# Hybrid conv / MLA / MoE step on one core: conditioning units moved ahead of the latent weights and of the sum of squares

## The reference, cut to what matters

```python
shift1, scale1, gate1, shift2, scale2, gate2 = split(silu(c_vec) @ w_ada + b_ada, 6)   # w_ada: 1024 x 6144
h = rms_norm(x, norm1) * (1 + scale1) + shift1
conv_in, q_lat, kv_lat, k_rope, gates = split_projection(h @ w_in)      # w_in: 1024 x 3488
...
x = x + gate1 * ((g_conv * conv_out + g_att * att) @ w_out)
h2 = rms_norm(x, norm2) * (1 + scale2) + shift2
x = x + gate2 * hier_moe(h2, ...)       # 16 experts in 4 groups, top 1 group, top 2 experts
```

## Time and profile before

| | |
|---|---|
| median of 3 runs | 1084.63 us (1083.62 to 1086.83) |
| the profiled execution's own time | 1087.17 us |
| its span (first to last instruction) | 1085.4 us |
| TensorE busy (PE) | 975.4 us, 90% |
| VectorE busy (DVE) | 758.0 us, 70% |
| ScalarE busy (ACT) | 514.9 us, 47% |
| chain that ended last, by engine | PE 79%, DVE 10%, issue 5%, ACT 4%, DMA 3% |
| mean granted TensorE clock | 0.934 |

### The profile page before, as it was taken

The page is one execution under the profiler, slowest core; times in us unless marked ns, Lnnn a source line. Parts: engine busy times, 40 slices in busy tenths (PEclk is TensorE's granted clock), DMA queues, the critical chain, the costliest instruction groups (busy, mean ns, idle before and its releaser), DMA issues.

```text
span 1085.4 us, 15630 instructions
## 1 busy us (share of the span) xinstructions
PE 975.4 (90%) x5962; PEld 812.6 (75%) x5962; DVE 758.0 (70%) x1187; ACT 514.9 (47%) x732; POOL 13.3 (1%) x15
## 2 busy tenths in 40 slices
PE   4599999998998798998958999998899969899997
PEld 1388699777997776786837968986699867678775
DVE  0655979556654688898866587975566367898895
ACT  0451633366323475666554244317543157656662
POOL 0100000000000000000010000000000000000000
PEclk8599999998998699999988999999999968999999
DMA  9765265401530776868366426550045047875861
GB/s 379 308 230 217 79 263 210 187 1 40 206 143 1 293 292 248 309 260 336 136 243 262 175 101 245 211 209 34 9 169 205 8 192 288 338 267 213 341 235 58
DMA packets 30249, 215.48 MB, mean 199 GB/s; under 512 B 3553, under 2 KB 3585, under 8 KB 4449
## 3 DMA queue, kind: packets, MB, share of 16 engines
q1 hardware_dynamic: 29808, 213.20, 51.4%
q0 software_dynamic: 368, 1.29, 0.3%
HBM read 212.75 MB, written 1.74 MB: 198 GB/s over the span
## 4 chain that ended last, share of the span: by engine, by line
PE 79%; DVE 10%; issue 5%; ACT 4%; DMA 3%; DVEq 0%; SPq 0%; ACTq 0%; another core or an unknown queue 0%
PE ps L723 56%; PE ps L710 6%; PE ps L734 4%; DMA ring<-wfirst 2%; PE ps L930 2%; PE ps L1024 2%; PE ps L978 2%; ACT w_hi L1332 2%; PE ps L701 1%; PE ps L851 1%; DVE w_lo L594 1%; PE ps L1108 1%; DVE x L1871 1%; DVE rs L1464 1%; PE ps L920 1%
## 5 line engine op out<-in xcount | busy, mean ns | idle before, releaser
L594 DVE TENSOR_TENSOR w_lo<-ring,w_hi 128x2048 fp32r<-128x2048 f32 x96 | 218.6, 2290 | 33.8 <-ACT w_hi L1332 30.4
L1332 ACT ACTIVATE w_hi<-ring 128x2048 fp32r<-128x2048 f32 x96 | 182.5, 1911 | 34.7 <-PE ps L723 30.5
L723 PE MATMUL ps<-h_hi,w_hi 128*128 128x384 f32 x512 | 174.8, 341 | 0.0
L723 PE MATMUL ps<-h_hi,w_lo 128*128 128x384 f32 x512 | 172.0, 336 | 0.0
L723 PE MATMUL ps<-h_lo,w_hi 128*128 128x384 f32 x512 | 171.9, 336 | 0.0
L589 DVE TENSOR_TENSOR w_lo<-ring,w_hi 128x2048 fp32r<-128x2048 f32 x44 | 100.4, 2290 | 50.7 <-ACT w_hi L583 50.7
L583 ACT ACTIVATE w_hi<-ring 128x2048 fp32r<-128x2048 f32 x44 | 83.6, 1909 | 69.1 <-DMA ring<-wpre 34.3
L1529 DVE SCALAR_TENSOR_TENSOR z<-u,par,z 128x399 f32<-128x399 f32 x180 | 104.7, 629 | 1.5
L723 PEld LDWEIGHTS ps<-h_hi,w_hi 128*128 128x128 f32 x512 | 96.1, 188 | 11.2 <-issue 10.4
L723 PE MATMUL ps<-w_hi,hg_hi 128*128 128x512 f32 x256 | 103.8, 405 | 0.0
L723 PE MATMUL ps<-w_hi,hg_lo 128*128 128x512 f32 x256 | 101.3, 396 | 0.0
(11 more groups left out here) (243 smaller groups left out, 1627.0 us busy)
## 6 DMA issues: line engine op xcount, KB each, us to landing
ring<-wpre SPq DMA_DIRECT2D x96, 1024.0 KB, 6.2
ring<-wmoe SPq DMA_DIRECT2D x96, 1024.0 KB, 5.4
ring<-wfirst SPq DMA_DIRECT2D x8, 1024.0 KB, 13.6
x<-x SPq DMA_DIRECT2D x1, 1536.0 KB, 15.5
x_out<-x SPq DMA_DIRECT2D x4, 384.0 KB, 2.3
par<-par_in POOLq DMA_DIRECT2D x3, 367.5 KB, 6.8
const<-const_in SPq DMA_DIRECT2D x1, 314.0 KB, 3.0
ckv_out<-ckvT POOLq DMA_DIRECT2D x2, 64.0 KB, 2.7
```

The costliest lines, as they stand in the source:

```text
L594: return nc.vector.tensor_tensor(out, whole, leading.bitcast(F32), ALU.subtract)
L723: m = mm(out, a, b, start=(start and i == 0 and j == 0), stop=(stop and i == n - 1 and j == 2))
L1332: af(w_hi[m % MOE_PLACES], slot(pre_slot(m)), ACT.Copy).then_inc(split_hi, 1)
```

## The change

The three first conditioning units go to the head of each layer's list, ahead of the two latent units; one is left behind these (before: four). On TensorE the first two are worked ahead of the sum of squares, the third behind it, and the fourth behind latent chunk 3 (before: one behind the sum, three behind chunks 1, 3 and 5). The first unit of a batch gets two waits: for the batch before to have left bank 7 (`adaT_taken`), and for the third of the MoE's last products to have been added (`x_moe`). Nothing on ScalarE or VectorE is changed, nor the number of units or of matmuls.

```diff
-ADA_HEAD = 4
+ADA_AHEAD = 3
+ADA_HEAD = 1
-LAT_ADA = (1, 3, 5)
+LAT_ADA = 3
@@ pre_stream
-    out = [("lat", 0), ("lat", 1)] + [("ada", next(ada)) for _ in range(ADA_HEAD)]
+    out = [("ada", next(ada)) for _ in range(ADA_AHEAD)] + [("lat", 0), ("lat", 1)]
+    out += [("ada", next(ada)) for _ in range(ADA_HEAD)]
@@ ada
-                    if kind == "next" and n == first_unit:
-                        wait_taken(pe, l, "o", TT - 1)
+                    if n == first_unit:
+
+                        pe.wait_ge(adaT_taken, batches_before(l, kind))
+                        if kind == "next":
+                            wait_taken(pe, l, "o", TT - 1)
+                        else:
+                            pe.wait_ge(x_moe, done * KD + (BACK_BANKS.index(ADA_BANK) + 1))
@@ the start of the layer on TensorE
+                ada(PRE[0])
+                ada(PRE[1])
                 square_sum(0)
 
-                units = adas_after("lat", 1)
-                ada(units[0])
+                ada(PRE[2])
                 outs = [begin("lat", t) for t in range(TT)]
...
-                    if c in LAT_ADA:
-                        ada(units[LAT_ADA.index(c) + 1])
+                    if c == LAT_ADA:
+                        for e in adas_after("lat", 1):
+                            ada(e)
```

## The result

The changed kernel takes 1091.23 us, median of 17 runs (1084.98 to 1101.42), against 1084.63 for the kernel before (17 runs, 1080.8 to 1096.08). The ratio is 1.0056, interval 1.0032 to 1.0080: slower by 6.1 us, 3.5 to 8.7. The profiled execution took 1101.42 us, 10 above the median and the longest of the 17, so totals are read beside a second profile (1089.4 us span).

A forecast was written before the change was run, and what follows sets the result against it. TensorE holds 79% of the chain; changes count where the chain leaves it or its work could go elsewhere. +7.56 - 2.00 - 2.00 = +3.56 us on the profiled 1087.17, or +0.33%; on median 1084.63 that gives 1088.2, range 1085.2 to 1091.0.

The forecast's parts named there:

- The landing, +7.56: First layer's start: the latent unit, fourth instead of first, lands 7.56 us later and delays the first latent matmul as much.
- The chunks, -2.00 each: Latent chunks, both layers: two of three conditioning units between chunks go, each saving 1.00 us, so -2.00 per layer.
- The two units ahead of the sum, and the queue behind, 0: Second layer's start and later transfers: units fit TensorE's idle time before the sum of squares, later landings hold nothing up; 0.
- Sharing of the engines: Rival, faster: six transfers land near one another, so list place hardly counts; only -4.00 us remains, 1080.6; chance 0.08.
- VectorE stopping TensorE: Rival, second layer: chunks wait for VectorE's h_lo (slack 0.77 us), so no gain there; +5.56, 1090.2; chance 0.10.
- TensorE waited for h_lo between chunks: Sign at the latent chunks: seeing this wait in the changed profile would show the forecast wrong; no size given.
- The sum of squares as the late one: Rival: the sum, now behind two units, becomes the root's last release; adds some 1 us, 1089.2; chance 0.02.
- The clock: Rival at the latent products: the clock's slow stretch falls otherwise, 1087.0 or 1089.4; chance 0.20, half to each side.

The follow-up runs named there:

- second set: The changed kernel unaltered, timed and profiled again against the kernel before: ratio 1.0036 (1.0011 to 1.0061).
- one unit alone: Kernel before with one conditioning unit ahead of the latent ones in the first layer's list only; one execution, span 1088.2 us.
- first only: Changed kernel with the second layer put back as before, first layer as changed: ratio 1.0057 (1.0022 to 1.0091), median 1091.32 us.
- list only: Changed kernel with both layers' lists as changed but TensorE's order as before: ratio 1.0057 (1.0017 to 1.0096), median 1091.84 us.
- the swap: Changed kernel with root before hi(0) on ScalarE and reciprocal before lo(0) on VectorE, first layer: ratio 0.9990 (0.9946 to 1.0034), median 1087.72 us.

## Why the prediction was right or wrong

**The forecast** was 1088.2 in 1085.2 to 1091.0, slower. The measured 1.0056 is 1090.7 on the median of before, inside; the second set's 1.0036 is 1088.5. Direction and mechanism stand. That the total lies so near is in part luck: the starts gave less loss than forecast, and stretches that the forecast put at nothing gave more.

**The landing, +7.56: right.** 7.43 to 7.62 between the profiles of the table, and one unit alone 2.4 to 2.6. Over 44 to 49 us the changed kernel's DMA moved 423 GB/s (424 before). The figure of about 358 GB/s in the Trainium skill's "DMA: Bandwidth & Descriptors" ("Where 436 GB/s comes from") would have made 8.8, an estimate; the landings 2.50 us apart (1.049 MB, 420 GB/s) decide against it here.

**The chunks, -2.00 each: too small.** This is the term that was mis-sized. The second layer's latent stretch went from 19.13 to 19.18 (six profiles) to 16.75 to 17.13 (five), 2.3 us for two units. The term took the unit's own 1.00 from the chain, but the unit also costs the restart on both its sides. Where the clock is full it can be read without the rest: from the start of the fifth chunk's first matmul to the start of the eighth's last it is 7.98 us with one unit in between and 6.78 without, in both layers and in every profile in which a unit stands ahead of the fifth chunk, so 1.20 a unit. In the first layer the same two units gave 2.4 to 3.6, since the moment at which the clock rises lies elsewhere there: 18 matmuls in front of the first unit took 6.64 and 5.60 us in two profiles of the kernel before. Where the gates of the first layer end, the changed kernel is thus 4.0 to 5.0 us late, counted from the first issue, and not 5.6.

**The two units ahead of the sum, and the queue behind, 0: right.** The second start's distance from sum to latent product was 7.82 or 7.83 in both kernels, and VectorE still waited 6.12 us behind the latent products of the first layer (9.73 before).

**The sum at the starts** is then +7.5 - 2.6 - 2.3 = +2.6 (means over the profiles with and without), not +3.56. What brings the measured ratio above it, 3.9 to 6.1 us, lies in stretches that the change doesn't touch. The second profile shows 2.0 us from the second glu on, 1.0 of it inside the attention whose clock fell (57.8 for 56.8 from mean product to output products) and 0.9 behind it (299.4 for 298.5); and up to 2.3 in the stretch to the second sum, where three of the six profiles with three units ahead in the first layer (the second changed one, first only, the changed one with twelve matmuls) have a fall at the first attention and none with another first start has. A short fall there made 1.0 of it (57.8 for 56.8); the two profiles of before differ by 1.3 in this stretch between them. That these falls make up the whole difference in the timed runs is argued. Of a timed execution the record has only the mean granted clock, with medians of 0.934 and 0.936 in the two sets of the changed kernel and of 0.934 to 0.937 in four of the kernel before, and these don't tell a short fall.

**The rivals.** Sharing of the engines: fell, the landings come in order. VectorE stopping TensorE: fell at the chunks that it was about, since the step to the third chunk was the plain 0.19 us. But the forecast's sign "TensorE waited for h_lo between chunks" came, at the second chunk, where the reading had missed it: `lo(1)` stands ahead of that chunk's h_lo. In the kernel before too the second chunk began at 51.72, 0.06 us behind its h_lo (50.92 + 0.74), after a step of 0.52 in place of 0.35. The wait is the same in both kernels, so it changes neither sum nor direction. The sum of squares as the late one: fell (list only). The clock was the right rival, but mostly at the wrong place. I had it as a toss between two lengths of the slow stretch at the latent products, where the Trainium skill's "TensorE: Matmul & The Clock Gate" ("What's actually happening") says the count of slow matmuls varies from run to run. The first layer agrees (6.64 and 5.60 us above), and its greater gain there is this rival come true in part. In the second layer it didn't vary: six profiles within 0.05 us. What the forecast didn't have came at the attention, went with when that begins, and in the changed kernel added time.

## What to carry to other kernels

A unit put ahead in a queue that is full delays all landings behind it by its whole transfer time (2.4 to 2.6 us here), which costs time only where the path waits for a landing; before moving work forward, look whether the path there runs through a landing (first layer) or through arithmetic (second layer), and give each its own order. An engine that makes something of a late landing before it does a small thing others wait for passes the delay on; here the swap gave 2.5 of 7.5 us back. What a unit between matmuls costs is read from the matmul steps around it, with and without it, not from its own length in the chain (1.20 against 1.00). And where a kernel has stretches in which the granted clock can fall, a shift of 2 us ahead of them can make or break a fall, as it did here, so read the untouched stretches too before explaining a total.

## What was not expected of the hardware

With the same work, an attention stretch of 33.7 us at granted clock 1.00 took 44.7 when the clock stayed at 0.50 for 27 of them. Between these, a short fall (748.4 to 751.8 us in the second changed profile) cost about 1.0 at once (mean product to output products 57.8 in place of 56.8). It came with the same attention code or not, by how long after the rise of the clock the stretch began: with twelve added matmuls it was gone from the changed kernel, with seven it was there in the kernel before, in one profile each. Where no fall comes in the attention, the time repeats to a tenth of a microsecond: glu to the end 493.00 to 493.10 us in five profiles of four kernels.
